# Two-block kernel on one core: where a scan's modulation rows and result products stand among its level products

## The reference

```python
mod = jax.nn.silu(c) @ ada_w[l] + ada_b[l]          # and the same for c_ctx
sh1, sc1, g1, sh2, sc2, g2 = [m[:, None, :] for m in jnp.split(mod, 6, axis=-1)]
...
def step(S, inp):                                    # wkv_scan, forward and reversed
    r_t, w_t, kk_t, b_t, v_t, k_t = inp
    sa = jnp.einsum("bhvk,bhk->bhv", S, kk_t)
    S = (S * w_t[:, :, None, :] - sa[..., None] * b_t[:, :, None, :]
         + v_t[..., None] * k_t[:, :, None, :])
    return S, jnp.einsum("bhvk,bhk->bhv", S, r_t)
...
x = x + g1 * out_x
hx = modulate(rms_norm(x, norm2_g[l]), sh2, sc2)
x = x + g2 * conv_ffn(hx, lp, rows, GRID_W)
```

## Time and profile before

| what | us |
|---|---|
| median of 3 runs | 1567.88 |
| the three runs | 1567.88, 1564.88, 1568.94 |
| the profiled execution | 1571.56 |
| its span | 1570.0 |
| TensorE's mean granted clock in it, share of full speed | 0.962 |
| steps -1 to 10 of the scan in it | about 245 to 529 |

### The profile page before, as it was taken

How to read it: one execution, slowest core, us unless ns; L and a number is a source line. 1 busy time by engine, 2 the same in 40 slices (tenths; PEclk the granted TensorE clock), 3 DMA queues, 4 the chain that set the end, 5 groups by cost and what they waited for, 6 DMA issues and landing times.

```text
span 1570.0 us, 35522 instructions
## 1 busy us (share of the span) xinstructions
PE 1489.1 (95%) x14858; PEld 1227.3 (78%) x14858; DVE 920.6 (59%) x1499; ACT 597.5 (38%) x1037; POOL 272.7 (17%) x290
## 2 busy tenths in 40 slices
PE   5999988999999989999999998998989999999997
PEld 3788865788899777887777887877878888888885
DVE  4424245588667748888886224767565655555222
ACT  4422344435342534444443223546664222322221
POOL 0000023565352010111111121000021111111110
PEclk9999997789879999999999999999999999999999
DMA  9232201233220222232223222221112232232221
GB/s 372 96 109 81 81 0 50 63 95 103 81 64 4 83 81 81 81 107 82 105 87 104 92 92 81 98 72 55 59 50 87 102 107 91 96 107 92 93 92 72
DMA packets 38987, 139.15 MB, mean 89 GB/s; under 512 B 3152, under 2 KB 3664, under 8 KB 38480
## 3 DMA queue, kind: packets, MB, share of 16 engines
q1 hardware_dynamic: 38720, 135.24, 25.4%
q10 hardware_dynamic: 144, 2.10, 0.3%
HBM read 135.22 MB, written 2.10 MB: 87 GB/s over the span
## 4 chain that ended last, share of the span: by engine, by line
PE 79%; DVE 13%; ACT 3%; issue 3%; DMA 1%; ACTq 0%; DVEq 0%; SPq 0%
PE bank L722 56%; PE bank L904 9%; DVE ffn_sb L3159 5%; PE bank L731 2%; PE bank L668 2%; PE bank L998 1%; DVE w_up L2587 1%; PE bank L1070 1%; PE bank L1010 1%; DMA arena<-w 1%; PE bank L935 1%; PE bank L661 1%; ACT w_up L1681 1%; ACT arena L2177 1%; DVE w_in L2587 1%
## 5 line engine op out<-in xcount | busy, mean ns | idle before, releaser
L722 PE MATMUL bank<-hf_hi,w_up 128*128 128x512 f32 x1376 | 424.0, 389 | 0.0
L722 PEld LDWEIGHTS bank<-hf_hi,w_up 128*128 128x128 f32 x1376 | 258.3, 188 | 53.2
L722 PE MATMUL bank<-hf_lo,w_up 128*128 128x512 f32 x688 | 269.1, 391 | 4.6 <-DVE w_up L2587 4.6
L722 PE MATMUL bank<-act_hi,w_down 128*128 128x512 f32 x704 | 216.7, 389 | 0.0
L904 PEld LDWEIGHTS bank<-arena 64*64 64x64 f32 x4224 | 161.1, 154 | 31.6 <-issue 19.3
L904 PE MATMUL bank<-arena 64*64 64x32 f32 (+1 forms) x4224 | 172.4, 237 | 7.8 <-DVE arena L2814 2.5
L1681 ACT ACTIVATE w_up<-ring 128x1024 fp32r<-128x1024 f32 x87 | 91.9, 1058 | 215.7 <-PE bank L722 215.7
L2587 DVE TENSOR_TENSOR w_up<-ring,w_up 128x1024 fp32r<-128x1024 f32 x87 | 106.8, 1229 | 97.0 <-ACT w_up L1681 97.0
L722 PEld LDWEIGHTS bank<-hf_lo,w_up 128*128 128x128 f32 x688 | 129.1, 188 | 36.1 <-DVE w_up L2587 8.8
L3159 DVE SCALAR_TENSOR_TENSOR ffn_sb<-ffn_sb 128x512 f32<-128x512 f32 x176 | 151.5, 861 | 5.4
L722 PEld LDWEIGHTS bank<-act_hi,w_down 128*128 128x128 f32 x704 | 132.1, 188 | 27.3
(11 more groups left out here) (350 smaller groups left out, 2388.8 us busy)
## 6 DMA issues: line engine op xcount, KB each, us to landing
ring<-w SPq DMA_DIRECT2D x76, 1024.0 KB, 4.8
ring<-w SPq DMA_DIRECT2D x32, 704.0 KB, 4.0
ring<-w SPq DMA_DIRECT2D x64, 256.0 KB, 3.0
arena<-w SPq DMA_DIRECT2D x8, 1024.0 KB, 18.2
x<-xT SPq DMA_DIRECT2D x1, 2048.0 KB, 10.2
x<-xT ACTq DMA_DIRECT2D x1, 2048.0 KB, 8.4
outT<-x SPq DMA_DIRECT2D x4, 512.0 KB, 2.7
arena<-ctxT SPq DMA_DIRECT2D x1, 1024.0 KB, 18.4
```

The lines of the kernel that those rows point to most:

```text
L722: ins = mm(out, w[:, a, k, :], of_block(b, k0 + k), start=first and k == 0 and m == 0, stop=last and k == n - 1 and m == 2)
```

## The change

It changes the order of calls in steps -1 to 10, and nothing else: no product, transfer or copy is added or left out.

- Step -1: both parts of the modulation rows go right behind `nx` of level 2. They stood behind `nx` of level 3 and behind `dx` of level 3.
- Steps 0 and 1: both parts go behind `nx(m, 1, 2)`. They stood before it and behind `state_terms(n, 1)`.
- Steps 2 to 6: the first part goes from before `dx(m, 1, 4)` to behind `nx(m, 0, 5)`, the second from there to behind `dx(m, 0, 5)`, and `ada_select` from before `nx(m, 1, 6)` to before `dx(m, 1, 6)`.
- Steps 7 to 10: `results(n, 0)` goes from before `nx(m, 0, 4)` to behind `nx(m, 0, 5)`, and `results(n, 1)` from behind `dx(m, 0, 4)` to behind `nx(m, 0, 6)`. DVE's `second_result(n, 0)` goes from before `x_out(m, 1, 4)` to before `w_out(m, 0, 6)`.
- ACT: `first_result(n, 1)` goes ahead of `ada_row_out(n)` and `state_padded(m, 1)`.

```diff
@@ PE, step -1 @@
             nx(m, 0, 2)
             nx(m, 1, 2)
+            ada_part(n, 0)
+            ada_part(n, 1)
             token_gate(1, 0)
...
             nx(m, 1, 3)
-            ada_part(n, 0)
             token_gate(3, 0)
...
             dx(m, 1, 3)
-            ada_part(n, 1)
             token_gate(4, 0)
@@ PE, steps 0 and 1 @@
+                nx(m, 1, 2)
                 ada_part(n, 0)
-                nx(m, 1, 2)
+                ada_part(n, 1)
                 dx(m, 0, 2)
...
                 state_terms(n, 1)
-                ada_part(n, 1)
                 dx(m, 1, 3)
@@ PE, steps 2 to 6 @@
                 results(n, 1)
-                ada_part(n, 0)
                 dx(m, 1, 4)
                 nx(m, 0, 5)
+                ada_part(n, 0)
+                nx(m, 1, 5)
+                dx(m, 0, 5)
                 ada_part(n, 1)
+                dx(m, 1, 5)
+                nx(m, 0, 6)
+                nx(m, 1, 6)
+                dx(m, 0, 6)
+                ada_select(n)
+                dx(m, 1, 6)
@@ PE, steps 7 to 10, a loop of its own @@
+                nx(m, 0, 4)
+                turned(m, 1)
+                nx(m, 1, 4)
+                dx(m, 0, 4)
+                dx(m, 1, 4)
+                nx(m, 0, 5)
+                results(n, 0)
                 nx(m, 1, 5)
                 dx(m, 0, 5)
                 dx(m, 1, 5)
                 nx(m, 0, 6)
-                ada_select(n)
+                results(n, 1)
                 nx(m, 1, 6)
@@ ACT @@
                 tok_out(m, 0)
+                first_result(n, 1)
                 ada_row_out(n)
                 state_padded(m, 1)
-                first_result(n, 1)
@@ DVE, steps 7 to 10 @@
-                second_result(n, 0)
                 x_out(m, 1, 4)
...
                 x_out(m, 1, 5)
+                second_result(n, 0)
                 w_out(m, 0, 6)
```

More of the change, by code:

```diff
@@ L1244, in _ @@
                 dx(m, 1, 6)
-            for n in range(NCC - 2, NC - 1):
+            for n in range(NCC - 2, 7):
                 m, q = n + 1, n + 2
@@ L1271, in _ @@
                 results(n, 1)
-                ada_part(n, 0)
                 dx(m, 1, 4)
                 nx(m, 0, 5)
+                ada_part(n, 0)
+                nx(m, 1, 5)
+                dx(m, 0, 5)
                 ada_part(n, 1)
+                dx(m, 1, 5)
[4 more added lines that the diff above has]
+                dx(m, 1, 6)
+            for n in range(7, NC - 1):
+                m, q = n + 1, n + 2
+                nx(m, 0, 2)
+                updates(n, 0)
+                nx(m, 1, 2)
+                scores(q, 0)
+                dx(m, 0, 2)
+                dx(m, 1, 2)
+                state_terms(n, 0)
+                if n == NC - 2:
+                    gate_products(0, 1)
+                updates(n, 1)
+                nx(m, 1, 3)
+                nx(m, 0, 3)
+                scores(q, 1)
+                dx(m, 1, 3)
+                turned(m, 0)
+                dx(m, 0, 3)
+                state_terms(n, 1)
+                if n == NC - 2:
+                    gate_products(1, 2)
+                nx(m, 0, 4)
[5 more added lines that the diff above has]
+                results(n, 0)
                 nx(m, 1, 5)
@@ L2947, in _ @@
                 y_last(m, 1)
-            for n in range(NCC - 2, NC - 1):
+            for n in range(NCC - 2, 7):
+                m, q = n + 1, n + 2
+                w_out(m, 0, 2)
+                running_sums(q + 1, 1)
+                running_sums(q + 1, 0)
+                w_out(m, 1, 2)
+                scores_out(q, 0)
+                x_out(m, 1, 2)
+                x_out(m, 0, 2)
+                x_turned(m, 0, 2)
+                x_turned(m, 1, 2)
+                w_out(m, 1, 3)
+                w_out(m, 0, 3)
+                state_out(n, 0)
+                scores_out(q, 1)
+                x_out(m, 0, 3)
+                x_out(m, 1, 3)
+                state_out(n, 1)
+                x_turned(m, 0, 3)
+                w_out(m, 0, 4)
+                first_level(q, 1)
+                x_turned(m, 1, 3)
+                w_out(m, 1, 4)
+                x_out(m, 0, 4)
+                first_level(q, 0)
+                x_turned(m, 0, 4)
+                second_result(n, 0)
+                x_out(m, 1, 4)
+                w_out(m, 0, 5)
+                x_turned(m, 1, 4)
+                w_out(m, 1, 5)
+                x_out(m, 0, 5)
+                x_turned(m, 0, 5)
+                x_out(m, 1, 5)
+                w_out(m, 0, 6)
+                x_turned(m, 1, 5)
+                w_out(m, 1, 6)
+                first_turned(q, 0)
+                y_last(m, 0)
+                first_turned(q, 1)
+                y_last(m, 1)
+                second_result(n, 1)
+                mod_out(n)
+            for n in range(7, NC - 1):
                 m, q = n + 1, n + 2
@@ L2997, in _ @@
                 second_result(n, 1)
-                mod_out(n)
             for c in range(2):
```

## The result

| | before | after |
|---|---|---|
| median of 12 runs, us | 1562.77 | 1569.48 |
| lowest and highest | 1555.77, 1569.63 | 1567.08, 1572.00 |
| ratio, 95% interval | | 1.0050 (1.0028 to 1.0073) |
| profiled execution, us | 1571.56 | 1567.08 |
| its span, us | 1570.0 | 1565.5 |

The changed kernel is slower by 0.5%, some 6.7 us. The two profiled executions say the opposite, 4.5 us faster, and that is the first thing to explain. The profile of before, 1571.56 us, is slower than each of the 12 runs of before, and that of the changed kernel is the fastest of its 12. With nine more runs the median of before went from 1567.88 to 1562.77 us. The changed kernel's time of 1569.48 us lies inside the forecast's range, but on the wrong side of no change: a small gain was forecast, and it is a loss that the interval keeps clear of 1.

A forecast was written before the change was run, and what follows sets the result against it. PE, busy 95% of the span, was taken as the bound, its clock falling in the scan. Terms -4.5 - 3.2 + 2.1 - 11.6 + 4.0 + 5.4 + 9.0 - 6.1 = -4.9 took 1571.56 to 1566.7 us; range 1561 to 1573.

The forecast's parts named there:

- The terms without the clock: PE's added waits: steps 2 and 3 +2.1, steps 7 to 10 +4.0, for POOL before two scores +5.4 us.
- POOL's two waits: Before the scores of steps 8 and 9, PE waits 2.7 us each for POOL: +5.4 us.
- The clock behind POOL's waits: At the scores of steps 8 and 9 the clock falls for about 10 us each: +9.0 us.
- The rival by which the clock stays up there: No clock fall behind POOL's waits, all else as forecast: 1557.7 us, chance 0.27.
- Steps -1 to 1: Joined modulation parts bring the clock back at about 252 in step -1 (-4.5) and 306 in step 1 (-3.2 us).
- the term for the ends of steps 2 to 6, -11.6: Shorter runs of small products leave one of five step ends cold, saving 11.6 us.
- the rival by which four of five ends stay cold: Ends of steps 2 to 6 go cold as before, the 11.6 is not gained: 1578.3 us, chance 0.20.
- The term for the end of step 7 (-6.1): The moved results cover the cold 13.65 us at the end of step 7, saving 6.1 us.
- The rival that the clock follows idle time alone: Products' places gain nothing and waits cost: 1592.1 us, or 1583.1 if the clock stays up there; chance 0.05.

The follow-up runs named there:

- e1: The kernel before, unchanged, run again: 1563.39 us, ratio 0.9994.
- e5: The changed kernel with three extra unread products on PE ahead of its wait for POOL in chunks 10 and 11: 1562.16 us.
- e4: The changed kernel with POOL's results_decayed put behind the eight products of erase_decayed and keys_decayed: 1557.07 us.
- e10: The changed kernel with the results back at level 4 in steps 7 and 8 alone: 1554.48 us.
- e7: The kernel before with the modulation parts moved in steps -1, 0 and 1 alone, and ACT's new order: 1557.39 us.
- e3: The changed kernel with steps 7 to 10 as before, so only the modulation rows are moved: 1555.27 us.
- e6: The kernel before with the modulation parts moved in steps 2 to 6 alone, and ACT's new order: 1563.95 us.
- e9: The version of e3 with DVE's two first_level calls in steps 2 to 6 behind both masks of level 4: 1556.33 us.
- e2: The kernel before with the change to steps 7 to 10 alone: 1574.65 us.
- e8: The version of e3 with the first modulation part back before dx(m, 1, 4) in steps 2 and 3: 1567.79 us.

## Why the prediction was right in the range and wrong in the sign

**The waits were right.** The terms without the clock were 2.1 + 4.0 + 5.4 = +11.5; the table leaves +11.5, which is closer than either number deserves. One by one: in steps 2 and 3 1.18 us each, less the 0.19 that each of them had before (for step 3), or 2.0 for 2.1; at POOL's two waits 3.37 + 2.82 = 6.2 for 5.4 (the prediction's own rows give POOL 5.8 us and not 5.9, and so 5.2; in step 7 POOL's products took 0.88 us each and not 0.79); in steps 8, 9 and 10 0.68, 0.68 and 0.43. In step 7 records are missing at that place, and `dx(8, 1, 4)` starts 1.45 us behind the one recorded before it, as it does in step 2 (1.40), so that some 1.2 us of wait is likely there. That is 3.0 for 4.0. At the end `y_mean` waits 2.02 us, where 1.29 were in e1; this was not in the sum.

**The clock behind POOL's waits was right.** 13.66 and 10.24 cold us, for "about 10" at each; 7 to 9 us by e5, for 9.0. The rival by which the clock stays up there falls: e5 differs from the changed kernel in this alone. So do the steps that lead there: the order of POOL (e4), and that only the results of steps 7 and 8 count (e10).

**Steps -1 to 1 were right.** Both parts in one piece end at 248.06 in the changed kernel, and the clock is back at 247.50, sooner than the 252 forecast. In step 1 it is back at 298.70, and the 306 forecast are not to be set beside this, since the whole step now starts 7.8 us earlier: the stretch is 13.66 us long, and 13.15 were forecast (292.85 to 306). PE there:

```profile
244.85 3.21 PE L668 MATMUL bank<-ring,siluc 128*32 128x256 f32 x32
247.99 1.13 PE L935 MATMUL bank<-arena 64*128 64x512 f32 x4
...
294.84 3.64 PE L668 MATMUL bank<-ring,siluc 128*32 128x256 f32 x32
298.41 2.19 PE L904 MATMUL bank<-arena 64*64 64x32 f32 x64
```

The sum was -7.7 and e7 measured -7.1. Inside it two errors cancel: the stretch of step -1 is 13.7 us shorter where 10 were forecast, worth 6.1 us for 4.5, and in step 2 a stretch of 10.24 us took the place of one of 6.83, worth 1.5 the other way.

**The step that failed is the term for the ends of steps 2 to 6, -11.6.** Their cold stretches did go in the changed kernel's profile, all of them; with the same move there are 0 in e3 and e10, 3.4 cold us in e5 and e6, and 6.8 in e4 and e9. So the mechanism held, and the rival by which four of five ends stay cold is out. But the term priced 34.1 cold us that one profiled execution had. Where these steps are as before, e1's profile has 23.9 there, behind steps 5 and 6 alone, e2's 6.8 and e7's 3.4. e6, which makes this move alone, gains 0.5 us where the prediction's terms for it make 9.5, and 3.6 by its clock. A stretch that stands in one execution and not in the next is not there to be saved at its full length. The prediction had seen this ("they can't be saved twice") and then took 1566.7 all the same, with nothing off the term. The term for the end of step 7 (-6.1) has the same fault, since e1's profile has no stretch there, but e2 as a whole came out as forecast.

**The base was the second half of it.** "About no change" was meant against 1567.88, the median of three runs, and three runs of a kernel whose executions lie between 1551 and 1575 us do not fix it: the next nine brought it down by 5.1 us. With terms measured against a typical run, 11.5 of waits, -7.1 in steps -1 to 1, -3.6 behind steps 2 to 6 and 7 to 9 behind POOL's waits, the sum is +7.8 to +9.8, for +6.7 measured. The forecast was a small difference between large terms, and one term sized by a single execution was enough to turn its sign. That 1569.48 us still came out within 3 us of the 1566.7 is luck in good part: the sum starts at 1571.56, 8.8 us above the median of before, and the terms of e6's part are 9.0 us too large the other way.

**The rival that the clock follows idle time alone** gave 1592 or 1583 and is out: by it the products' places gain nothing, and e7 gains 7.1 us by them alone. In the first cold stretch PE is idle for 2.2 us in before and for 2.4 us in e7 (6.83 - 4.41), and yet the clock is back 13.7 us sooner. The Trainium skill (TensorE: Matmul & The Clock Gate, "HAM oscillation — how this bites in real kernels") names idle gaps as what brings the clock down. Here it is not idle time alone: in the changed kernel the clock falls at 448.88 in a wait of 3.37 us, and there the trace agrees, and in e3 it falls at 448.40 under a PE that is busy for 13.66 of 13.66 us:

```profile
448.40:462.06 13.66, 13.66 (x240) 13.17 (x236) 8.36 (x19) 4.46 (x15) 6.99 (x9) 0.50 0.01 3
```

## What to carry to other kernels

Before a gain is counted from a profile, look whether that execution is a typical one: set its time and mean granted clock against the runs, and price a cold stretch in full only where a second profile has it at the same place. When work is moved later, ask of each engine's order what stands behind the semaphore that this work gives: here a product that nobody needed soon held back eight that were needed at once. A filler put back before one level of a bound chain only moved the wait to the next (e8); what it is worth depends on where the clock then falls, and that has to be run.

## What the runs showed of the hardware

**The spread of the runs goes with the clock.** In 35 runs of before, 1551.3 to 1575.2 us, the correlation of time and mean granted clock is -0.88, and that of e1's twelve -0.97. The changed kernel's 12 runs lie within 4.9 us, those of before within 13.9. Why is open: e2 has the same two waits for POOL, and its runs spread over 13.6 us.

**Copies on DVE are slower beside POOL's products.** The same 12 copies of 64 by 128 from 430 to 520 us, busy us and mean ns, in the changed kernel:

```profile
L2840 DVE COPY_PREDICATED arena<-k_,arena 64x128 f32<-64x128 uint32 x12 | 5.2, 435 | 0.1
```

And in e4:

```profile
L2840 DVE COPY_PREDICATED arena<-k_,arena 64x128 f32<-64x128 uint32 x12 | 8.5, 709 | 0.1
```

They take 435 ns with POOL idle or waiting and 709 ns on the mean in e4, where POOL's products run beside those of steps 7 and 8; single ones took up to 0.98 us. That is 3.3 us more, on the chain that PE waits for. The same stands in steps 2 and 3 of the changed kernel. There the two copies ahead of the mask take 1.32 us, with POOL's products beside them from 330.74 on:

```profile
330.74 4.72 POOL L2406 TENSOR_TENSOR arena<-arena 64x256 f32<-64x256 f32 x6 [0.17 <-POOL arena L2406]
```

In steps 8 and 9, with POOL waiting, such a pair takes 0.89 us, and PE's wait before `dx(m, 1, 4)` is 0.68 us and not 1.18. The Trainium skill (SBUF — State Buffer, "SBUF: two separate sides") says that DVE operations with two inputs in SBUF and GpSimd's share one pair of ports, which one of them holds for a whole instruction. These copies read a mask and data, and the trace agrees in that they are slower beside POOL's products; which of the two held the ports, and for how long, it doesn't show.
